# Expert gathers of a two-block transformer kernel: u and v of an index in turn, without pauses, in groups of four

## The chip, the core and the metric

The kernel runs on one core of a Trainium2 chip. The metric is the device time of one execution in microseconds. All arrays are float32.

## What is computed

Two transformer blocks run one after the other over 256 tokens of width 1024. The first ends in a product-key expert layer (PEER), the second in a mixture of 32 experts. The change touches the PEER layer alone:

```python
def one_block(hb):                                   # 128 tokens
    q = (hb @ w_q).reshape(128, 8, 2, 128)
    sc = einsum('thcd,hcnd->thcn', q, sub_keys)      # 8 heads, 2 halves, 128 keys
    s1, i1 = top_k(sc[:, :, 0], 16); s2, i2 = top_k(sc[:, :, 1], 16)
    cand_s = (s1[..., :, None] + s2[..., None, :]).reshape(128, 8, 256)
    top_s, pos = top_k(cand_s, 16)
    idx = i1 * 128 + i2 at pos                       # 16 of 16384 experts
    g = softmax(top_s)
    act = gelu(einsum('thkd,td->thk', u_tab[idx], hb))
    return einsum('thk,thkd->td', g * act, v_tab[idx])
```

For each of 2 tiles of 128 tokens, 8 heads and 16 choices k, every token needs one row of 4 KB of u_tab and one of v_tab: 256 gathers of each table, 128 rows (0.5 MB) each, 268 MB in all.

## The kernel before

**Stages.** One program: block one with its weights streamed by SP (SyncE) through five slots of a ring in SBUF (a slot is 16 KB a partition, a unit 2 MB), the gather stage, block two with more units through the same slots, and last the experts, whose weights are streamed too. The units are numbered in the order of loading; unit n goes to slot n mod 5, and the last five of block one (four of w_peer_q, one of sub_keys) lie in slots 0 to 4 while TensorE computes the scores for the search. A sixth slot is not used by units then.

**Gather stage.** The order is written out by hand on each engine, and engines meet only in semaphores. A head of a tile is g = 8 tile + head; two heads make a pair, `par` is the head in the pair. Everything runs in program order on its engine:

- POOL (lines 681 to 712) waits for the indices of a head (`s_route`), copies them to `idx_now`, tells so (`s_taken`), issues the 16 u gathers and then the 16 v gathers, one indirect DMA each. A u gather waits until the dot on its row buffer is done (`s_dot`; eight buffers), a v gather until TensorE has used its buffer (`s_pv`; sixteen buffers). Ahead of each k with k % 4 == 2 POOL sets a small tile `spacer` to zero and waits for it (lines 695 to 696 and 705 to 706). The v gathers of the first head wait for the last use of ring slots 1 to 4 by block one (line 703), the u gathers from k = 4 on for that of slot 0.
- DVE (lines 1762 to 1800) forms the dot of each gathered u row with the token's row (`dot_rows`, one instruction per k over 1024 elements, line 1766), multiplies gelu by the softmax weight (`weights`), and does the search for the next pair in between: `best_keys` (two rounds of the eight best of 128, line 1558) behind the weights of the first head, `route` (sums, two rounds of the eight best of 256, indices, softmax, line 1576) behind those of the second. The search of the very first head comes before any dot, that of the second between its dots and weights.
- ACT (lines 1293 to 1325) computes gelu over a head's 16 dots, 16 diagonal matrices with the weights on the diagonal (line 1303), and the exponentials for the softmax. Before it come its copies for block one, the last of them the scores of key 7.
- TensorE (lines 908 to 919) waits for the 16 diagonals of a head (`s_diag`), then for each v gather, and adds diagonal times v rows to two PSUM banks: two matmuls of 512 columns for each k.
- SP (lines 616 to 628) loads the first unit of block two into slot 0 when all 256 dots are done (line 619), and the next four when the v rows in their slots have been used.

## Time and profile before

| | us |
|---|---|
| median of 3 runs | 2437.82 |
| lowest and highest run | 2437.38, 2440.33 |
| span of the profiled execution | 2439.8 |
| busy: TensorE, weight loads | 2067.6, 1173.3 |
| busy: DVE, ACT, POOL | 981.6, 552.4, 519.0 |
| 256 gathers of u on POOL, line 698: busy, mean of one | 240.9, 0.941 |
| 256 gathers of v on POOL, line 708: busy, mean of one | 244.2, 0.954 |
| 256 dots on DVE, line 1766: busy, mean of one | 312.5, 1.221 |
| 256 diagonals on ACT, line 1303: busy | 76.5 |
| matmuls on gathered rows, line 905, x1024: busy, mean of one | 480.7, 0.633 |

How to read it: the slices of the page cut the span in 40 parts of 61 us each; a digit is the tenth of the slice in which an engine was busy. PE is TensorE, PEld its weight load, SP is SyncE. The gathers go through the software queue q0, the loads of weights through the hardware queue q1, and both are served by the same 16 DMA engines. The span is 2.0 us above the median of the runs.

### The profile page before, as it was taken

The page shows a single profiled execution, that of the slowest core. Times are in us where ns is not written, and L with a number is a line of the kernel's source. Part 1 is how long each engine was busy: PE and PEld are TensorE (multiplying, and loading weights), DVE is VectorE, ACT ScalarE, POOL GpSimd, SP SyncE. Part 2 cuts the span into 40 slices and gives each one's busy share as a digit, 9 for nine tenths or more (in the row PEclk, how much of TensorE's full clock was granted, in tenths as well). Part 3 has the DMA queues.
Part 4 walks back from the last instruction along what each step waited for, and adds up shares of the span by engine and source line. Part 5 has one row for each costly group of instructions (what it writes and reads, how often), then busy time and mean ns, then how long its engine had stood idle before and what let it go on. Part 6 is the DMA issues. An engine that isn't in the chain of part 4 may idle for free.

```text
span 2439.8 us, 27459 instructions
## 1 busy us (share of the span) xinstructions
PE 2067.6 (85%) x8940; PEld 1173.3 (48%) x8941; DVE 981.6 (40%) x2190; ACT 552.4 (23%) x1000; POOL 519.0 (21%) x688
## 2 busy tenths in 40 slices
PE   8999999757746756755899969999999999999997
PEld 7777888423322322322478854444444444444443
DVE  5955555465665576464065341111111111111113
ACT  4635201221011112011214222222222222222221
POOL 0000002466666666666100000000000000000000
PEclk9999999978878877887999979999999999999999
DMA  7352585699999999999633318699999999999995
GB/s 293 138 207 81 214 359 208 248 362 361 360 352 369 358 364 354 358 349 369 248 138 139 142 74 366 257 430 429 428 428 429 428 428 429 428 429 428 429 429 219
DMA packets 111686, 784.32 MB, mean 321 GB/s; under 512 B 13040, under 2 KB 13296, under 8 KB 80144
## 3 DMA queue, kind: packets, MB, share of 16 engines
q1 hardware_dynamic: 37904, 515.18, 51.0%
q0 software_dynamic: 73728, 268.47, 29.7%
q8 instruction: 28, 0.46, 0.1%
q14 instruction: 26, 0.21, 0.0%
HBM read 782.55 MB, written 1.05 MB: 321 GB/s over the span
## 4 chain that ended last, share of the span: by engine, by line
PE 47%; issue 2%; DVE 1%; DMA 1%; ACT 1%; DVEq 0%; POOL 0%; ACTq 0%; POOLq 0%
PE ps L746 42%; PE ps L905 3%; PE ps L1104 1%; DMA ring<-in_peer_v,arena 1%; PE ps L1135 0%; PE ps L1136 0%; DVE arena L1806 0%; PE ps L1061 0%; DVE ring L2054 0%; ACT arena L1344 0%; DVE arena L2056 0%; DVE ring L2055 0%; ACT arena L1416 0%; ACT arena L1341 0%; DVE arena L1808 0%
## 5 line engine op out<-in xcount | busy, mean ns | idle before, releaser
L746 PE MATMUL ps<-ring,arena 128*64 128x512 f32 (+2 forms) x3336 | 748.4, 588 | 44.4 <-issue 40.5
L905 PE MATMUL ps<-ring,arena 128*128 128x512 f32 x1024 | 480.7, 633 | 266.1 <-issue 187.7
L746 PEld LDWEIGHTS ps<-ring,arena 128*64 128x64 f32 (+1 forms) x3336 | 263.0, 140 | 502.6 <-issue 498.1
L746 PE MATMUL ps<-arena,ring 128*128 128x256 f32 x2208 | 492.5, 382 | 8.6 <-ACT arena L1353 3.7
L905 PEld LDWEIGHTS ps<-ring,arena 128*128 128x128 f32 x1024 | 206.8, 204 | 538.7 <-issue 530.8
L746 PEld LDWEIGHTS ps<-arena,ring 128*128 128x128 f32 x2208 | 419.3, 191 | 75.3 <-issue 13.6
L1766 DVE CUSTOM_DVE_ANT_0 ring<-ring,ps 128x1024 f32<-128x1024 f32 x256 | 312.5, 1221 | 241.1 <-DMA ring<-in_peer_u,arena 226.1
L2027 DVE TENSOR_TENSOR arena<-ps,arena 128x512 f32<-128x512 f32 x66 | 45.7, 692 | 647.6 <-PE ps L1104 647.6
L1456 ACT COPY arena<-ps 128x512 f32<-128x512 f32 (+1 forms) x198 | 108.4, 548 | 728.3 <-PE ps L746 672.2
L708 POOL DMA_INDIRECT ring<-in_peer_v,arena x256 | 244.2, 954 | 135.8 <-issue 105.0
L698 POOL DMA_INDIRECT ring<-in_peer_u,arena x256 | 240.9, 941 | 130.2 <-issue 74.8
L746 PE MATMUL ps<-arena 128*128 128x128 f32 (+6 forms) x1486 | 222.6, 306 | 28.2 <-DVEq L2003 13.6
L746 PEld LDWEIGHTS ps<-arena 128*128 128x128 f32 (+2 forms) x1486 | 197.4, 198 | 45.6 <-issue 21.8
L1295 ACT ACTIVATE arena<-arena 128x16 f32<-128x16 f32 x16 | 4.9, 308 | 569.2 <-issue 318.6
L690 POOL COPY arena<-arena 128x16 uint32<-128x16 uint32 x16 | 3.3, 203 | 390.3 <-POOLq L689 390.2
L1303 ACT ACTIVATE arena<-arena 128x128 f32<-128x128 f32 x256 | 76.5, 388 | 5.6 <-DVE arena L1773 3.4
L905 PE MATMUL ps<-arena 64*128 64x512 f32 (+2 forms) x312 | 75.2, 579 | 2.6 <-ACTq L1430 1.0
L1527 DVE CUSTOM_DVE_ANT_0 ring<-ring,arena 128x1024 f32<-128x1024 f32 x48 | 56.0, 1222 | 3.1 <-DVE arena L1680 0.7
L1832 DVE SCALAR_TENSOR_TENSOR arena<-arena 128x256 f32<-128x256 f32 x120 | 50.2, 481 | 1.6
L1819 DVE TENSOR_SCALAR arena<-arena 128x128 f32 (+1 forms) x68 | 18.5, 288 | 78.4 <-issue 73.4
L727 POOL MEMSET arena<- 128x128 f32 x1 | 0.2, 205 | 216.5 <-DVEq L1941 216.5
L1456 ACT ACT_TABLE_LOAD x33 | 42.3, 1283 | 16.3 <-ACT arena L1456 15.2
(332 smaller groups left out, 1101.3 us busy)
## 6 DMA issues: line engine op xcount, KB each, us to landing
ring<-in_w_exp SPq DMA_DIRECT2D x192, 2048.0 KB, 17.1
ring<-in_w_in SPq DMA_DIRECT2D x24, 2048.0 KB, 8.3
ring<-in_w_ada SPq DMA_DIRECT2D x12, 2048.0 KB, 8.9
ring<-in_w_out SPq DMA_DIRECT2D x4, 2048.0 KB, 7.8
ring<-in_w_peer_q SPq DMA_DIRECT2D x4, 2048.0 KB, 12.4
ring<-in_w_br_rnn SPq DMA_DIRECT2D x4, 1280.0 KB, 9.5
ring<-in_w_br_attn SPq DMA_DIRECT2D x2, 2048.0 KB, 13.8
ring<-in_peer_u,arena POOLq DMA_INDIRECT x256
```

The lines of the kernel that those rows point to most:

```text
L698: pool.indirect_dma_start(out=u_rows[k % 8], out_offset=None, in_=a["peer_u"], in_offset=bass.IndirectOffsetOnAxis(ap=idx_now[:, par, k:k ...
L708: pool.indirect_dma_start(out=v_gath[k], out_offset=None, in_=a["peer_v"], in_offset=bass.IndirectOffsetOnAxis(ap=idx_now[:, par, k:k + 1] ...
L746: return pe.matmul(o, l, r, start=start, stop=stop)
L905: return pe.matmul(o, l, r, start=start, stop=False, skip_group_check=True)
L1104: last = pe.transpose(ps[:, EXPERT_BANK[job], j * P:(j + 1) * P], z_sb[:, n, j * P:(j + 1) * P], ident)
L1303: last = fn(diag[:, par, k, :], ident, ACT.Copy, scale=wts[:, par, k:k + 1])
L1456: own(act.copy(dst, src))
L1527: own.mark(dve.tensor_tensor_reduce(w[:, j, :], w[:, j, :], c_row, 1.0, 0.0, ALU.mult, ALU.add, mod[:, m:m + 1]))
L1766: dve.tensor_tensor_reduce(u_rows[k % 8], u_rows[k % 8], h2_rows[tile], 1.0, 0.0, ALU.mult, ALU.add, dots[:, par, k:k + 1]).then_inc(s_dot, 1)
L1819: own.mark(ts(dst[:, t, :], numbers, slot_of[:, t, at_e], None, ALU.is_equal))
L1832: own.mark(stt(conv[:, c, :], src, w, conv[:, c, :], ALU.mult, ALU.add))
L2027: own(tt(dst.rearrange("p j (h s) -> p j h s", h=2), ps[:, bank, :].rearrange("p (j h s) -> p j h s", j=4, h=2), bias.unsqueeze(3).to_broa ...
```

## The change

A gather buffer is now a pair of 8 KB: u in its first half, v in its second, in sixteen slots instead of eight u buffers and sixteen v buffers. Twelve of the pairs lie in the ring, four in the arena. POOL issues u and v of an index one behind the other, both counting on one semaphore of that slot (`uv_full`), with a single wait (TensorE has used the slot) and no spacer. DVE, ACT and TensorE work in groups of four k: four dots, gelu, weights, four diagonals, eight matmuls. The search is cut into six pieces that stand behind the dots and before the weights of a group. The very first two heads are searched one by one before any dot. SP loads each unit of block two when the two pairs in its ring slot have been used by the last head. Work per gather, dot, diagonal and matmul is the same.

```diff
+GROUP = 4
-        carve("P", CR, T)
+        hole = carve("P", CR * T)
-        spacer = carve("P", 2 * TOPK)
-        u_rows = [ring[:, i * D:(i + 1) * D] for i in (20, 21, 22, 23, 0, 1, 2, 3)]
-        v_gath = [ring[:, (4 + i) * D:(5 + i) * D] for i in range(16)]
+        in_ring = [ring[:, i * 2 * D:(i + 1) * 2 * D] for i in range(12)]
+        in_arena = [hole[:, 0:2 * D]] + [carve("P", 2 * D) for _ in range(3)]
+        uv_rows = in_ring[10:12] + in_ring[0:2] + in_arena + in_ring[2:10]
+        ring_place = {0: 2, 1: 8, 2: 10, 3: 12, 4: 14}
+        n_groups = TOPK // GROUP
# SP
-                if n == n_first:
-                    sp.wait_ge(s_dot, 8 + TT * PH * TOPK)
-                elif n < n_first + RING:
-                    sp.wait_ge(s_pv, 17 + TT * PH * TOPK - 4 * (RING - 1 - n % RING))
+                if n < n_first + RING:
+                    sp.wait_ge(s_pv, 17 + (TT * PH - 1) * TOPK + ring_place[n % RING] + 2)
# POOL
                         for k in range(TOPK):
+                            for s, place in ring_place.items():
+                                if k == place:
+                                    unit_free(pool, last_in_slot(s, n_first))
                             if k == 4:
-                                unit_free(pool, last_in_slot(0, n_first))
-                            if k % 4 == 2:
-                                own(pool.memset(spacer, 0.0))
-                            own.mark(pool.wait_ge(s_dot, i * (2 * TOPK) + TOPK * g + k + 1))
-                            pool.indirect_dma_start(
-                                out=u_rows[k % 8], ..., in_=a["peer_u"], ...).then_inc(u_full[k % 8], 16)
-                        for s in range(1, RING):
-                            unit_free(pool, last_in_slot(s, n_first))
-                        for k in range(TOPK):
-                            if k % 4 == 2:
-                                own(pool.memset(spacer, 0.0))
+                                A.filled(pool, "ss2")
                             own.mark(pool.wait_ge(s_pv, i * (2 * TOPK) + TOPK * g + k + 2))
-                            pool.indirect_dma_start(
-                                out=v_gath[k], ..., in_=a["peer_v"], ...).then_inc(v_full[k], 16)
+                            pool.indirect_dma_start(out=uv_rows[k][:, 0:D], ..., in_=a["peer_u"],
+                                                    in_offset=at_k).then_inc(uv_full[k], 16)
+                            pool.indirect_dma_start(out=uv_rows[k][:, D:2 * D], ..., in_=a["peer_v"],
+                                                    in_offset=at_k).then_inc(uv_full[k], 16)
# TensorE
-                        pe.wait_ge(s_diag, i * 2 + g + 1)
                         for k in range(TOPK):
-                            pe.wait_ge(v_full[k], i * 32 + 16 * (g + 1))
+                            if k % GROUP == 0:
+                                pe.wait_ge(s_diag, i * (2 * n_groups) + g * n_groups + k // GROUP + 1)
# ACT
             for tile in range(TT):
                 if tile == 0:
-                    gelu_dots(0, 0, 0)
                     act.wait_ge(s_soft_in, 2)
                     fn(top_s[:, 1, :], top_s[:, 1, :], ACT.Exp).then_inc(s_soft, 1)
...
                 with act.Fori(1 - tile, PH // 2 - tile) as i:
                     for par in range(2):
-                        gelu_dots(tile, par, i)
-                        diagonals(tile, par, i)
+                        for j in range(n_groups):
+                            gelu_dots(tile, par, j, i)
+                            diagonals(tile, par, j, i)
+                        if par == 0:
+                            next_exponentials(i + tile * (PH // 2) + 1)
# DVE, first two heads
-            best_keys(0, slice(0, 1))
-            route(0, slice(0, 1))
+            for h in range(2):
+                head = slice(h, h + 1)
+                best_keys(0, 0, head); best_keys(0, 1, head); best_pairs(0, head); best_pairs(1, head)
...
+                soften(0, head); part_of_route(0, head); part_of_route(1, head); give_route(head)
+                normalise(1 + h, head)
# DVE, dots of a group
+                for k in range(j * GROUP, (j + 1) * GROUP):
+                    dve.wait_ge(uv_full[k], i * 64 + 32 * (g + 1))
+                    last = dve.tensor_tensor_reduce(uv_rows[k][:, 0:D], uv_rows[k][:, 0:D], h2_rows[tile], ...,
+                                                    dots[:, par, k:k + 1])
+                last.then_inc(s_dots, 1)
# DVE, first pair of tile 0: head 1
+                    dot_rows(0, 1, 0, 0); best_keys(1, 0); best_keys(1, 1); weights(0, 1, 0, 0)
+                    dot_rows(0, 1, 1, 0); best_pairs(0); best_pairs(1); soften(1); weights(0, 1, 1, 0)
+                    dot_rows(0, 1, 2, 0); part_of_route(0); weights(0, 1, 2, 0)
+                    dot_rows(0, 1, 3, 0); part_of_route(1)
                     dve.wait_ge(s_taken, 2)
+                    give_route(); weights(0, 1, 3, 0); normalise(3)
# DVE, loop over the other pairs
+                    dot_rows(tile, 0, 0, i); best_keys(after, 0); weights(tile, 0, 0, i)
+                    dot_rows(tile, 0, 1, i); best_keys(after, 1); weights(tile, 0, 1, i)
+                    dot_rows(tile, 0, 2, i); best_pairs(0); weights(tile, 0, 2, i)
+                    dot_rows(tile, 0, 3, i); best_pairs(1); soften(after); weights(tile, 0, 3, i)
+                    dot_rows(tile, 1, 0, i); part_of_route(0); weights(tile, 1, 0, i)
+                    dot_rows(tile, 1, 1, i); part_of_route(1)
                     dve.wait_ge(s_taken, i * 2 + tile * PH + 2)
+                    give_route(); weights(tile, 1, 1, i)
+                    for j in (2, 3):
+                        dot_rows(tile, 1, j, i); weights(tile, 1, j, i)
+                    normalise(after + 2)
```

(Statements that stand on lines of their own in the kernel are joined by ";" here. `best_keys(p, half)` and `best_pairs(half)` find the first or the second eight of sixteen, `part_of_route(c)` turns a position into the key of half c, `give_route` writes the indices for POOL, `soften` and `normalise` are the two sides of the softmax around ACT's exponential.)

## Rows read from the trace of the kernel before

**Rows 1.** Slices of the page, 40 over the span: two engines, bytes moved.
```profile
PE   8999999757746756755899969999999999999997
POOL 0000002466666666666100000000000000000000
GB/s 293 138 207 81 214 359 208 248 362 361 360 352 369 358 364 354 358 349 369 248 138 139 142 74 366 257 430 429 428 428 429 428 428 429 428 429 428 429 429 219
```
**Rows 2.** Windows: length, busy PE, PEld, DVE, ACT, POOL (count), clock, DMA share, GB/s.
```profile
480.00:1080.00 600.00, 382.20 (x832) 166.02 (x831) 367.23 (x864) 86.80 (x244) 406.12 (x527) 0.82 0.97 359
1160.00:1167.00 7.00, 7.00 (x18) 3.11 (x17) 0.00 (x0) 0.00 (x0) 3.99 (x6) 1.00 1.03 415
1500.00:2400.00 900.00, 859.86 (x4514) 385.73 (x4510) 153.55 (x341) 198.06 (x279) 0.00 (x0) 1.00 0.98 417
```
**Rows 3.** Timeline of POOL, 502 to 517 us: start, duration, instruction, [idle before it].
```profile
502.87 0.14 POOL L706 MEMSET arena<- 128x32 f32 x1
503.81 0.94 POOL L708 DMA_INDIRECT ring<-in_peer_v,arena  x1 [0.80 <-issue]
505.05 0.94 POOL L708 DMA_INDIRECT ring<-in_peer_v,arena  x1 [0.30 <-issue]
...
510.79 0.93 POOL L708 DMA_INDIRECT ring<-in_peer_v,arena  x1 [0.30 <-issue]
511.72 0.21 POOL L690 COPY arena<-arena 128x16 uint32<-128x16 uint32 x1
512.83 0.97 POOL L698 DMA_INDIRECT ring<-in_peer_u,arena  x1 [0.91 <-issue]
...
516.07 0.94 POOL L698 DMA_INDIRECT ring<-in_peer_u,arena  x1 [0.88 <-POOLq L697]
```
**Rows 4.** Waits of POOL, 466 to 1166 us: total, times, longest.
```profile
POOL ring L708 <- PE ps L905: 4.7, 9, 0.8
POOL ring L698 <- DVE arena L1766: 4.2, 8, 0.9
```
**Rows 5.** Timeline: first u gather and first dot of heads 1 and 15.
```profile
466.46 0.97 POOL L698 DMA_INDIRECT ring<-in_peer_u,arena  x1 [0.90 <-issue]
471.73 1.22 DVE L1766 CUSTOM_DVE_ANT_0 ring<-ring,ps 128x1024 f32<-128x1024 f32 x1 [18.30 <-DMA ring<-in_peer_u,arena]
...
1120.78 0.97 POOL L698 DMA_INDIRECT ring<-in_peer_u,arena  x1 [0.90 <-issue]
1126.12 1.22 DVE L1766 CUSTOM_DVE_ANT_0 ring<-ring,ps 128x1024 f32<-128x1024 f32 x1 [22.09 <-DMA ring<-in_peer_u,arena]
```
**Rows 6.** Queues from 1160 to 1167 us, the only one with packets.
```profile
q0 software_dynamic: 794, 2.90, 102.8%
```
**Rows 7.** End of the stage: timeline of ACT, POOL and PE, and one window.
```profile
1150.39 4.78 ACT L1303 ACTIVATE arena<-arena 128x128 f32<-128x128 f32 x16 [0.24 <-issue]
1164.77 0.94 POOL L708 DMA_INDIRECT ring<-in_peer_v,arena  x1 [0.30 <-issue]
1187.25 6.44 PE L905 MATMUL ps<-ring,arena 128*128 128x512 f32 x8 [3.58 <-DMA ring<-in_peer_v,arena]
1188.00:1192.00 4.00, 4.00 (x6) 1.67 (x5) 0.00 (x0) 0.00 (x0) 0.00 (x0) 0.50 0.04 17
1206.37 29.64 PE L746 MATMUL ps<-arena,ring 128*128 128x256 f32 x128 [3.70 <-ACT arena L1353]
```
**Rows 8.** DVE: the dots (min, median, max ns), search of a pair (windows).
```profile
L1766 DVE CUSTOM_DVE_ANT_0 ring<-ring,ps x256: 1220/1221/1223, 399.1 to 1148.5; 128x1024 f32<-128x1024 f32 x128
681.50:694.95 13.45, 11.48 (x35) 0.65 0.96 365
447.10:453.45 6.35, 5.89 (x35) 0.63 0.87 312
```
**Rows 9.** Start of the stage, timeline: first u and v gathers, DVE's wait.
```profile
394.51 1.13 POOL L698 DMA_INDIRECT ring<-in_peer_u,arena  x1 [1.07 <-POOLq L697]
443.24 0.94 POOL L708 DMA_INDIRECT ring<-in_peer_v,arena  x1 [26.05 <-PE ps L746]
446.28 0.17 DVE L1611 TENSOR_REDUCE arena<-arena 128x1 f32<-128x16 f32 x1 [10.15 <-ACT arena L1310]
```

234 lines of the change are left out of this document (140 added, 94 removed).

## Prediction

> **What bounds the kernel now.** I read the slices of the page first. POOL is busy only in slices 7 to 20, and there TensorE drops to 4 to 7 tenths while the GB/s line stands near 360 [rows 1]. This is the gather stage, some 790 us of the span; the stages behind it wait for its result, so what it loses or gains moves the end one for one. By the windows, DVE is busy 61%, PE 64% at a granted clock of 0.82, ACT 14% and POOL 68% between 480 and 1080 us [rows 2]. No compute engine is full. That leaves the transfers, and the question on which everything rests is whether the 16 DMA engines or POOL's issuing sets their pace. The DMA share of 0.97 in the same row suggests the engines.
>
> The timeline of POOL says otherwise. A plain step from one gather to the next is 0.94 for the instruction and 0.30 of idle time, 1.245 by the starts. A spacer makes it 0.94 + 0.14 + 0.80 = 1.88 ahead of a v gather and 1.96 ahead of a u gather (0.88 idle), and the copy of the next head's indices 0.93 + 0.21 + 0.91 = 2.05 [rows 3]. A head's 32 gathers make 23 plain steps, 4 + 4 with a spacer, and 1 copy: 28.6 + 7.8 + 7.5 + 2.0 = 46.0 us; the first gathers of two heads start at 466.46 and 512.83, 46.4 apart [rows 3, 5]. POOL hardly waits for slots: 4.7 us for PE and 4.2 for DVE in 700 us [rows 4]. And the gathers land soon: the first u gather of a head is issued at 466.46 and, 14 heads later, at 1120.78, its dot starts at 471.73 and 1126.12: 5.3 us later both times [rows 5]. A queue that were too slow for its issuer would fall behind over 650 us; this one does not. So POOL, with its pauses, sets the pace and the DMA engines follow.
>
> How fast they could go is seen once. From 1160 to 1167 the gathers queue up behind a weight load, the hardware queue is silent, and the software queue alone moves 2.90 MB at 415 GB/s, while POOL still issues [rows 2, 6]. A gather is 128 rows of 4 KB, 0.524 MB: 1.26 us at 415 GB/s, against 1.46 at the stage's 359. The high DMA share at 359 GB/s is then packets that wait for work with their clock running; that is my inference.
>
> Here a rule of the Trainium skill speaks against the change. The page "HBM Reference" (its table of bandwidths) gives an effective 358 GB/s per core, half of a stack's 716, and the stage sits on that figure; it adds that a core that streams alone measures about 425. By the first figure nothing is to be had from faster issuing. By that rule the trace disagrees: 415 GB/s for gathers, 417 for the expert weights [rows 2]. The rule is one of the rivals below, with its time from rows.
>
> **The change part by part.** The sum runs from the first gather of the second head to the end of the stage; before, that gather is issued at 466.46 and the last one, 479 steps later, at 1164.77 [rows 5, 7]: 698.3 us, 1.458 each.
>
> *Pauses gone, u and v in turn.* A head has 31 plain steps and one copy: 31 x 1.245 + 2.05 = 40.6 us, 1.27 a gather. The steps of before add up to 46.0 a head, yet 698.3 x 32 / 479 is 46.65, so 0.6 a head (0.02 a gather) is irregular; I keep it: 1.29. One wait for two gathers instead of one each may shorten the 0.30 or not; the bounds are 0.94 (no gap) and 1.245, and I take 1.245, since that is what all plain steps show. The DMA floor is 1.26, so a faster POOL would gain only down to that. 479 x 1.29 = 617.9 us: 80.4 less. In all 16 slots a gather now finds one free: a pair is held from issue to landing (5.3), until its group of four has landed (up to three pairs, 7.7), for a dot (1.22 [rows 8]), a piece of search (up to 4), gelu and weights (0.7, between the last dot and the first diagonal), four diagonals (4.78 / 4 = 1.2 [rows 7]) and at most 8 matmuls (6.4 at 1.2 GHz [rows 7]): 27 us, against 41 until the slot's turn comes again.
>
> *Start.* Today u gathers of head 0 go out from 394.51, and the v gathers stand still until 443.24 for the last ring slot [rows 9]. The new order fills four arena slots and slot 5 and 0 at once and takes the others as TensorE leaves them (400 to 443): head 0 is fully issued by about 447, 17 us sooner than 465.36. But DVE now searches both heads before its first dot, and the second normalise waits for an exponential that ACT issues only behind its last key copy: today DVE stands there until 446.28 [rows 9]. ACT has the first gelu less ahead of it, so the dots start at about 446. Four dots (5.0), gelu and weights (0.7), diagonals (1.3) and the first pair of matmuls (1.6 at 1.2 GHz) free the first slot: head 1's first gather at 455, **11.5 us earlier** than 466.46. POOL is idle for some 8 us before it. DVE then needs 5.7 us per uncovered group, which is under the 10.3 that POOL needs to issue one.
>
> *The first routes.* In the first pair of heads the next route is given only behind the last dots of head 1. Head 1 is issued from 455 to 495.5; its last pair lands near 500, a dot and the second half of the routing (3 + 0.6 us by the sum of its rows, [rows 8]) put the route at 504, and POOL needs it at 496: **+8 us**, once. In the loops the route comes two groups earlier, ahead of POOL's need.
>
> *Search in pieces.* The same instructions as before: 6.3 us of keys and 13.3 of pairs and routing for two heads [rows 8]. With 32 dots of 1.25 that is 60 us of DVE per 81 us of gathers. Each piece is 2.9 to 4 us and stands behind four dots, 9 us of a group's 10.3. Covered at no cost; if the gathers came at 1.15 us each, the cover would be gone.
>
> *End.* Today SP has asked for four weight units by the time the last gather is issued, and they share the queue with it: issue at 1164.77, matmul at 1187.25, 22.4 us where the steady lag is 5.3 [rows 5, 7]. Now slot 0's load starts behind the first group of the last head and the others behind the third and fourth, so one unit of 2 MB (5.1 us at 415 GB/s) lies beside the last gathers: 10.4 us, **12 us less**. The next stage reads the units from 12.7 us after the last matmul (1206.37 - 1193.69), one per 7.4 (29.64 / 4) [rows 7], and four units take about 20 us at 417 GB/s, the first of them under way by then; it should not wait. Behind the last landing come now a dot, gelu, weights, four diagonals and 8 matmuls: 1.25 + 0.7 + 1.3 + 6.4 = 9.7, against 6.5 today [rows 7]: **+3**.
>
> Sum: -80.4 - 11.5 + 8 - 12 + 3 = **-93 us**. The profiled execution's span is 2439.8; the median of the runs is 2437.8, 2 us under it. I carry the difference over: 2437.8 - 93 = **2345 us**. Its own range goes by the pace: 1.266 (the DMA floor) and no wait for routes give -20, so 2325; 1.34 gives +24, so 2369.
>
> **The rivals.**
>
> *A. The ceiling of the stage is HBM's.* Then gathers stay at the 359 GB/s of the stage, 1.46 each, and only start and end gain: 479 x 1.46 = 699, so +1 - 11.5 + 4 (half of the route's wait is covered by a backlog) - 12 + 3 = -15.5: **2422 us**. For it: a steady 360 GB/s in all slices. Against it: the 415 GB/s and the constant lag. The page named above says this for a core whose neighbour is busy.
>
> *B. POOL or the loop is slower than the bare steps.* DVE's search and POOL's descriptor writing meet more often, or the hand-offs DVE, ACT, DVE, ACT, PE of each group hold slots longer than 27 us. A pace of 1.38 gives 479 x 0.09 = 43 more: **2388 us**. For it: 0.6 us a head are irregular already. Against it: POOL's waits for PE and DVE add up to 9 us.
>
> *C. Slower: two tables in turn.* Today 16 gathers in a row read one table, now each reads the other one at the same indices; no stretch of the trace does that, and none shows a queue kept full for longer than some 10 us. If a full, alternating queue moves less, all 479 steps pay. It decides from 1.29 + 93 / 479 = 1.484 us, 353 GB/s, on; at 330 GB/s (1.59) it is 479 x 0.30 - 93 = +51: **2489 us**. Against it I have only that DMA served 415 GB/s behind a backlog, of one table.
>
> *D. The pauses go and nothing moves,* since POOL is held by slots at just the old pace: needs a hold of 46 us, 19 more than my sum. 2437 us.
>
> **How the numbers follow.** My forecast 0.70, B 0.12, A 0.09, C 0.06, D 0.03. Forecast and B reach from 2325 to about 2400 and hold 0.82; I give 2323 to 2402. The kernel can be told from no change from about 0.2%, 5 us. Faster: forecast, B, A, 0.90 after rounding for what I have not thought of; same 0.03; slower 0.07.
>
> **What the profile would show.** The first test is the step of POOL's timeline: 1.245 throughout with 2.04 at each head, and 40.6 to 41.3 us from one copy of indices to the next. GB/s in the stage: 405 or more in my case, 375 to 395 in B, near 360 in A with gathers much longer than 0.94 us or POOL waiting for PE, under 353 in C. DMA idle for some 5 to 8 us before 460 and again near 500. The last matmul near 1100 instead of 1193.7. TensorE in the stage: bursts of 8 matmuls with pauses, the granted clock at or under 0.82, much of it at 1.2 GHz; harmless as long as 8 matmuls (6.4 us) fit in a group's 10.3. The prediction fails if the lag from issue to landing grows while POOL waits for slots: then the engines, not POOL, set the pace.

## The result, and the profile after

The kernel after takes **2347.2 us** (median of 4 runs, 2346.5 to 2348.0), the kernel before 2437.7: a ratio of 0.9631, with an interval of 0.9618 to 0.9644. That is 90.5 us less. The profiled execution's span is 2345.1, 94.7 under that of before.

The page of after: its head, three lines of the slices, the groups of gathers and dots, and the median time from issue to landing of the u gathers (last line; its last number).

```profile
span 2345.1 us, 27078 instructions
PE 2090.4 (89%) x8940; PEld 1175.9 (50%) x8941; DVE 977.5 (42%) x2238; ACT 569.1 (24%) x1046; POOL 499.9 (21%) x560
PE   8999999868877777876999889999999999999996
POOL 0000002557777777773000000000000000000000
GB/s 305 140 213 64 179 358 254 288 330 410 410 410 409 409 409 410 410 407 379 108 144 108 144 217 257 420 429 429 428 428 428 429 429 429 428 428 428 429 429 215
L1790 DVE CUSTOM_DVE_ANT_0 ring<-ring,ps 128x1024 f32<-128x1024 f32 x192 | 231.9, 1220 | 153.5 <-DMA ring<-in_peer_v,arena 153.0
L699 POOL DMA_INDIRECT ring<-in_peer_u,arena x192 | 182.7, 951 | 87.4 <-issue 47.3
L701 POOL DMA_INDIRECT ring<-in_peer_v,arena x192 | 179.9, 937 | 59.8 <-issue 55.8
ring<-in_peer_u,arena POOLq DMA_INDIRECT x192, 6.8
```

Against [rows 1] the GB/s line of the gather stage stands at 409 to 410 where it wandered between 349 and 369, the stage is a slice and a half shorter, and PE works at 7 to 8 tenths in it. Gathers and dots cost what they cost before: 0.94 to 0.95 and 1.22 us each. Only the idle time between them went.

Windows of after (length, busy PE, PEld, DVE, ACT, POOL, granted clock, DMA share, GB/s), the stage without its ends; it answers to the first line of [rows 2].

```profile
500.00:1060.00 560.00, 430.57 (x875) 179.13 (x874) 369.73 (x898) 102.58 (x289) 413.90 (x449) 0.89 1.01 404
```

Timeline of POOL in after, at the change from one head to the next; it answers to [rows 3].

```profile
829.30 0.94 POOL L701 DMA_INDIRECT ring<-in_peer_v,arena  x1 [0.30 <-issue]
830.24 0.21 POOL L689 COPY arena<-arena 128x16 uint32<-128x16 uint32 x1
831.43 0.97 POOL L699 DMA_INDIRECT ring<-in_peer_u,arena  x1 [0.99 <-POOLq L697]
832.71 0.94 POOL L701 DMA_INDIRECT ring<-in_peer_v,arena  x1 [0.31 <-issue]
833.95 0.93 POOL L699 DMA_INDIRECT ring<-in_peer_u,arena  x1 [0.30 <-PE ps L895]
```

The plain step is 833.95 - 832.71 = 1.24, as before, and the one with the copy 831.43 - 829.30 = 2.13 (2.05 before). From 451.31, the first gather of head 1, to 1075.66, the last of all, the 479 steps take 624.35 us. One stop of 11.9 us is in it, so the pace is 612.5 / 479 = 1.279 us.

Start of the stage in after: DVE's wait for the last exponential, the first dot, TensorE's first group and head 1's first gather. It answers to [rows 9] and the first lines of [rows 5]. The last line is the first route that POOL has to wait for: its idle time of 11.87 us is the stop.

```profile
439.51 0.17 DVE L1625 TENSOR_REDUCE arena<-arena 128x1 f32<-128x16 f32 x1 [34.66 <-ACT arena L1306]
440.38 1.22 DVE L1790 CUSTOM_DVE_ANT_0 ring<-ring,ps 128x1024 f32<-128x1024 f32 x1 [0.22 <-issue]
446.93 8.71 PE L895 MATMUL ps<-ring,arena 128*128 128x512 f32 x16 [5.69 <-ACT arena L1296]
451.31 0.97 POOL L699 DMA_INDIRECT ring<-in_peer_u,arena  x1 [5.68 <-POOLq L697]
...
502.67 0.20 POOL L689 COPY arena<-arena 128x16 uint32<-128x16 uint32 x1 [11.87 <-DVEq L1540]
```

End of the stage in after, timeline; it answers to [rows 7].

```profile
1075.66 0.94 POOL L701 DMA_INDIRECT ring<-in_peer_v,arena  x1 [0.31 <-issue]
1089.14 1.22 DVE L1790 CUSTOM_DVE_ANT_0 ring<-ring,ps 128x1024 f32<-128x1024 f32 x1 [1.25 <-DMA ring<-in_peer_v,arena]
1092.27 7.13 PE L895 MATMUL ps<-ring,arena 128*128 128x512 f32 x16 [1.59 <-ACT arena L1296]
```

The last matmul of the stage ends at 1092.27 + 7.13 = 1099.4, where it was 1193.7: all of the gain lies ahead of this point. What comes behind it takes 1245.7 us of the span, and took 1246.1.

One thing to know before comparing start times between executions: the first gather of all, which comes right behind block one and the first head's search, starts at 394.51 in before and at 392.54 in after. From that gather to the end of the span it is 2045.3 us in before and 1952.6 in after, 92.7 less.

### The profile page after: what moved, and what is told of

Same layout as the page of the kernel before. It is cut to its first block, busy times and chain, and to the rows that moved or that the text cites. A ratio compares the mean times of both kernels' runs of the same rounds, so it can differ in the third digit from the quotient of the medians.

```text
span 2345.1 us, 27078 instructions
## 1 busy us (share of the span) xinstructions
PE 2090.4 (89%) x8940; PEld 1175.9 (50%) x8941; DVE 977.5 (42%) x2238; ACT 569.1 (24%) x1046; POOL 499.9 (21%) x560
## 4 chain that ended last, share of the span: by engine, by line
PE 71%; POOL 7%; DMA 7%; issue 6%; DVE 6%; ACT 3%; DVEq 0%; POOLq 0%; ACTq 0%; SPq 0%
PE ps L736 58%; PE ps L895 10%; DMA ring<-in_peer_v,arena 4%; POOL ring L699 2%; POOL ring L701 2%; DMA arena<-in_peer_v,arena 2%; PE ps L1095 1%; POOL arena L699 1%; POOL arena L701 1%; ACT arena L1296 1%; DVE ring L1790 1%; DMA ring<-in_sub_keys 0%; DVE arena L1740 0%; ACT arena L1241 0%; PE ps L1126 0%
## 5 line engine op out<-in xcount | busy, mean ns | idle before, releaser
L895 PE MATMUL ps<-ring,arena 128*128 128x512 f32 x768 | 389.9, 667 | 125.8 <-ACT arena L1296 125.8
L895 PEld LDWEIGHTS ps<-ring,arena 128*128 128x128 f32 x768 | 160.9, 215 | 352.4 <-issue 194.2
L1790 DVE CUSTOM_DVE_ANT_0 ring<-ring,ps 128x1024 f32<-128x1024 f32 x192 | 231.9, 1220 | 153.5 <-DMA ring<-in_peer_v,arena 153.0
L736 PE MATMUL ps<-arena 128*128 128x128 f32 (+6 forms) x1486 | 220.9, 304 | 28.1 <-DVEq L2059 13.6
L895 PE MATMUL ps<-arena 64*128 64x512 f32 (+2 forms) x568 | 194.1, 597 | 26.3 <-ACT arena L1296 23.7
L699 POOL DMA_INDIRECT ring<-in_peer_u,arena x192 | 182.7, 951 | 87.4 <-issue 47.3
L701 POOL DMA_INDIRECT ring<-in_peer_v,arena x192 | 179.9, 937 | 59.8 <-issue 55.8
L895 PEld LDWEIGHTS ps<-arena 128*128 128x128 f32 (+1 forms) x568 | 78.0, 191 | 118.1 <-issue 77.8
L1790 DVE CUSTOM_DVE_ANT_0 arena<-arena,ps 128x1024 f32<-128x1024 f32 x64 | 76.7, 1220 | 34.0 <-DMA arena<-in_peer_v,arena 33.4
L699 POOL DMA_INDIRECT arena<-in_peer_u,arena x64 | 60.7, 948 | 19.5 <-issue 15.6
L701 POOL DMA_INDIRECT arena<-in_peer_v,arena x64 | 60.2, 940 | 19.5 <-issue 19.2
## 6 DMA issues: line engine op xcount, KB each, us to landing
ring<-in_w_peer_q SPq DMA_DIRECT2D x4, 2048.0 KB, 10.4
```

What stands on the lines that cost most here:

```text
L699: pool.indirect_dma_start(out=uv_rows[k][:, 0:D], out_offset=None, in_=a["peer_u"], in_offset=at_k).then_inc(uv_full[k], 16)
L701: pool.indirect_dma_start(out=uv_rows[k][:, D:2 * D], out_offset=None, in_=a["peer_v"], in_offset=at_k).then_inc(uv_full[k], 16)
L736: return pe.matmul(o, l, r, start=start, stop=stop)
L895: return pe.matmul(o, l, r, start=start, stop=False, skip_group_check=True)
L1790: last = dve.tensor_tensor_reduce(uv_rows[k][:, 0:D], uv_rows[k][:, 0:D], h2_rows[tile], 1.0, 0.0, ALU.mult, ALU.add, dots[:, par, k:k + 1])
```

## The experiments

**1. The pauses alone.** The kernel before, with its layout, its two tables one behind the other and its groups of sixteen, without the spacer.

> The kernel before with nothing changed but the eight spacers per head taken out of POOL's stream: u buffers, v buffers, the run of 16 u gathers and then 16 v gathers, whole heads and the unbroken search stay. Theory P (the pauses alone set the pace): a head takes 31 x 1.245 + 2.05 = 40.6 to 41.3 us instead of 46.4, so 479 steps x (1.458 - 1.28) = 85 us less: 2353 us, between 2347 and 2362. Rival L (pairs in slots, turns and groups are needed to keep DVE, ACT and PE up with faster gathers): POOL waits for its eight u buffers or its v buffers, a head takes 44 us or more, 2400 us or more.

```diff
-                per = 2 * (2 + 2 * TOPK + 2 * TOPK // 4)
+                per = 2 * (2 + 2 * TOPK)
...
-                            if k % 4 == 2:
-                                own(pool.memset(spacer, 0.0))
...
-                            if k % 4 == 2:
-                                own(pool.memset(spacer, 0.0))
```

Measured: **2356.5 us** (2351.8 to 2358.1, 4 runs), ratio 0.9657 (0.9636 to 0.9678). Slices of this kernel (bytes moved) and the largest of its waits of POOL in the stage (total, times, longest):

```profile
GB/s 304 115 215 86 164 367 254 233 409 408 402 410 410 409 408 400 410 400 355 112 140 108 146 188 261 420 429 428 428 429 428 428 429 429 428 428 429 429 428 210
...
POOL ring L696 <- DVE arena L1762: 14.5, 42, 2.0
```

Eight small instructions a head, taken out of POOL's stream, give 81 of the 90.5 us, and up to 410 GB/s with them. Pairs, turns, groups and the search in pieces are worth some 9 us together.

Where the 9 us lie can be read from the two traces. The old layout costs little in the steady state: the 479 steps from head 1's first gather on take 616.2 us here and 612.5 in after without its stop, 4 us more. (The 14.5 us that POOL waits for one of the eight u buffers, where it waited 4.2 [rows 4], say less than they seem to: each of these waits holds the 0.30 us of idle time that every plain step has, 42 times here and 8 times there.) Head 1 starts 66.9 us after the first gather of all, where it is 58.8 in after, and after loses these 8 us again, and more, in its stop before head 2, which this kernel doesn't have. What is left is the end: from the last issue to the end of the span it is 1278.3 us here and 1269.5 in after, 9 less.

**2. The pauses put back.** The kernel after, with a spacer ahead of every fourth gather.

> The changed kernel with eight spacers per head put back (one behind every four gathers); all else as changed. Theory P: a head takes 40.65 + 8 x 0.70 = 46.2 us, 479 steps grow by 0.17 each, +80 us: 2427 us, between 2415 and 2436. Rival L (the layout and groups carry the gain): within 20 us of the changed kernel, 2347 to 2367.

```diff
+        spacer = carve("P", 2 * TOPK)
...
-                per = 2 * (2 + TOPK)
+                per = 2 * (2 + TOPK + TOPK // 2)
...
+                            if k % 2 == 1:
+                                own(pool.memset(spacer, 0.0))
```

Measured: **2428.8 us** (2424.6 to 2433.8, 10 runs), ratio 0.9965 (0.9954 to 0.9976). A window of the stage, the spacer with the gather behind it, and the page's median from issue to landing:

```profile
500.00:1040.00 540.00, 382.05 (x743) 157.75 (x741) 324.75 (x815) 89.10 (x246) 361.08 (x470) 0.85 0.96 353
...
700.93 0.15 POOL L699 MEMSET arena<- 128x32 f32 x1
701.98 0.94 POOL L702 DMA_INDIRECT ring<-in_peer_u,arena  x1 [0.90 <-POOLq L700]
...
ring<-in_peer_u,arena POOLq DMA_INDIRECT x192, 5.6
```

Seen from this side the pauses are 81.6 us, and everything else 8.9. The two experiments agree within the scatter of the runs, so the parts add up: no sign that they help or hinder one another.

**3. The turns undone.** The layout and the groups of after, with sixteen u gathers and then sixteen v gathers into the same slots; DVE waits for u alone, TensorE for v, once a group.

> The changed kernel, but POOL issues the 16 u gathers of a head and then its 16 v gathers, into the same slots; DVE waits for u alone, TensorE for the v rows of a group of four. Theory P: the order of the two tables costs and gives nothing; POOL still steps by 1.245, a slot is held for about 20 + 5.3 + 3.7 + 6.4 = 35 us of the 41 until its turn, so 2347 within 6 us. Rival T (rival C of the prediction in either direction: turns between the two tables at one index change what the DMA engines move): a difference of more than 10 us at a GB/s in the stage other than 404, with the lag from issue to landing changed by over 1 us.

```diff
-        uv_full = [sem(f"uv_rows_loaded_{k}") for k in range(TOPK)]
+        u_full = [sem(f"u_rows_loaded_{k}") for k in range(TOPK)]
+        v_full = [sem(f"v_rows_loaded_{j}") for j in range(TOPK // GROUP)]
...
                             pool.indirect_dma_start(out=uv_rows[k][:, 0:D], out_offset=None, in_=a["peer_u"],
-                                                    in_offset=at_k).then_inc(uv_full[k], 16)
+                                                    in_offset=at_k).then_inc(u_full[k], 16)
+                        for k in range(TOPK):
+                            at_k = bass.IndirectOffsetOnAxis(ap=idx_now[:, par, k:k + 1].bitcast(U32), axis=0)
                             pool.indirect_dma_start(out=uv_rows[k][:, D:2 * D], out_offset=None, in_=a["peer_v"],
-                                                    in_offset=at_k).then_inc(uv_full[k], 16)
+                                                    in_offset=at_k).then_inc(v_full[k // GROUP], 16)
...
+                            if k % GROUP == 0:
+                                pe.wait_ge(v_full[k // GROUP], i * (2 * 16 * GROUP) + 16 * GROUP * (g + 1))
...
-                    dve.wait_ge(uv_full[k], i * 64 + 32 * (g + 1))
+                    dve.wait_ge(u_full[k], i * 32 + 16 * (g + 1))
```

Measured: **2364.5 us** (2363.5 to 2366.4, 4 runs), ratio 0.9699 (0.968 to 0.9718): 17 more than after, where I had expected no difference. A window, head 1's first gather, POOL's waits from there on, and the page's median from issue to landing:

```profile
500.00:1040.00 540.00, 386.82 (x844) 167.86 (x842) 357.94 (x895) 101.00 (x284) 389.36 (x422) 0.86 1.01 397
...
464.07 0.97 POOL L700 DMA_INDIRECT ring<-in_peer_u,arena  x1 [0.97 <-POOLq L698]
...
POOL ring L700 <- PE ps L898: 25.4, 49, 0.8
...
ring<-in_peer_u,arena POOLq DMA_INDIRECT x192, 6.0
```

Head 1's first gather starts 12.8 us later than in after (10.7 counted from the first gather of all), since no v gather of head 0 can go out before all its u gathers, and those need the last ring slot. The stop before head 2 is 8.6 us shorter in return. The rest are waits of POOL for slots: a slot now waits from its u gather until its v gather, sixteen steps later, has landed and been used. In heads 1 to 15 some 38 gathers have more idle time before them than the plain 0.30, mostly 0.78 and 17 us too much together; in after it is one gather, 1.3 us. So the turns are worth something by how long a slot is held and by an earlier start. That the DMA engines should care which table comes next, rival C, has nothing for it: the 397 GB/s are fewer than the 403 of after over the same window, but gathers land sooner (6.0 against 6.8 us), so it is POOL that issues less and not the queue that is slower.

**4. Fewer bytes.** The kernel after, with v gathers of 512 columns (half rows of a view of the table with 2 KB rows); both halves of the result are formed from them. Part of the computation is thus changed, and a quarter of the bytes of the stage is gone. The number of gathers, dots and matmuls is the same.

> The changed kernel with v gathers of 512 columns (rows of 2 KB out of the table seen as twice as many rows) in place of 1024; TensorE multiplies the same 512 columns for both halves of the output, so the output is another one. Bytes of the stage fall by a quarter. Theory P: POOL's steps are the bound, every head takes 40.65 instead of 40.65 to 41.9 us (mean 41.0), the stage is some 5 us shorter and the end 3 us: 2339 us, between 2333 and 2344. Rival D (the DMA engines at some 410 GB/s hold the stage and POOL is kept back by them): with 0.39 MB per gather on average the pace could fall towards 1.0 us and the time by 20 us or more, 2325 or less.

```diff
-                            pool.indirect_dma_start(out=uv_rows[k][:, D:2 * D], out_offset=None, in_=a["peer_v"],
+                            pool.indirect_dma_start(out=uv_rows[k][:, D:D + 512], out_offset=None, in_=a["peer_v"].rearrange("n (h c) -> (n h) c", h=2),
...
-                            add(ps[:, 2 * tile + 1, :], diag[:, par, k, :], uv_rows[k][:, D + 512:2 * D])\
+                            add(ps[:, 2 * tile + 1, :], diag[:, par, k, :], uv_rows[k][:, D:D + 512])\
```

Measured: **2345.9 us** (2342.9 to 2348.2, 4 runs), ratio 0.9616 (0.9596 to 0.9637), 1.3 under after and not to be told from it. The window of the stage, its slices, and the median from issue to landing:

```profile
500.00:1040.00 540.00, 411.02 (x847) 171.62 (x847) 359.31 (x883) 99.83 (x280) 399.55 (x430) 0.90 0.89 301
...
GB/s 305 113 215 90 155 378 230 209 263 307 304 311 298 309 307 306 305 300 340 108 144 108 144 217 259 420 428 429 428 428 428 429 428 429 429 428 429 428 428 211
...
ring<-in_peer_u,arena POOLq DMA_INDIRECT x192, 4.8
```

With the load of the engines down from 404 to 301 GB/s the stage is as long as before. So POOL's own issuing is a bound too. The few us that I had expected to come back did not: I had put the irregular 0.6 us of a head down to the engines, and they are not theirs. The GB/s line says it as well: it wanders from 298 to 311, as it wandered in [rows 1], where POOL set the pace, while after's stands still at 409 to 410.

The traces also show where much of the irregular part is. A few gather instructions last 1.0 to 1.4 us on POOL instead of 0.94: 9 of them in heads 1 to 15 of after, 14 in this experiment. Every one of the 9 stands beside instructions of DVE's search, 7 of them beside its operations on 128x512 elements; none of the 358 gathers that a dot overlaps in after is one of them. Timeline of after:

```profile
572.36 0.69 DVE L1609 TENSOR_TENSOR arena<-arena 128x512 f32<-128x512 f32 x1
572.59 1.28 POOL L699 DMA_INDIRECT ring<-in_peer_u,arena  x1 [0.31 <-issue]
573.13 0.69 DVE L1611 TENSOR_TENSOR arena<-arena 128x512 f32<-128x512 f32 x1
```

That the search causes them is not shown by an experiment; they fit the first half of rival B, at a small price (3 us in all in after).

**5. Groups undone on DVE.** In the loops (12 of the heads) the weights of a head are formed only behind its sixteen dots, in the layout of after.

> The changed kernel, but in the loops (6 of 8 pairs of heads) DVE forms the weights of all four groups only behind the last dots of the head and the search pieces; pairs in slots, turns, no pauses stay. Theory H (a slot holding u and v is given back late unless diagonals follow each group): the first slot is held from issue for 38 (15 pairs issued) + 5.3 (landing) + 1.25 (dot) + up to 4 (piece) + 0.7 + 1.3 + 1.6 = 48 to 52 us against the 41 of its turn, POOL waits for PE, some 50 us a head in 12 heads: 2347 + 12 x 9 = 2455 us, between 2425 and 2485, slower than the kernel before. Rival N (groups bring nothing, POOL's steps decide): 2347 within 5 us.

```diff
                     best_keys(after, 0)
-                    weights(tile, 0, 0, i)
                     dot_rows(tile, 0, 1, i)
...
-                    weights(tile, 0, 3, i)
+                    for j in range(n_groups):
+                        weights(tile, 0, j, i)
...
-                    weights(tile, 1, 1, i)
-                    for j in (2, 3):
-                        dot_rows(tile, 1, j, i)
+                    dot_rows(tile, 1, 2, i)
+                    dot_rows(tile, 1, 3, i)
+                    for j in range(n_groups):
                         weights(tile, 1, j, i)
```

Measured: **2512.7 us** (2509.4 to 2514.4, 4 runs), ratio 1.0309 (1.0292 to 1.0325): slower than the kernel before by 75 us, 58 more than I had put on it. Timeline of a head's end: the last dot, the first weights, the first diagonals and POOL's next gather.

```profile
549.80 1.22 DVE L1790 CUSTOM_DVE_ANT_0 ring<-ring,ps 128x1024 f32<-128x1024 f32 x1 [1.26 <-DMA ring<-in_peer_v,arena]
553.63 0.16 DVE L1797 TENSOR_TENSOR arena<-arena 128x4 f32<-128x4 f32 x1 [0.21 <-issue]
553.91 1.28 ACT L1296 ACTIVATE arena<-arena 128x128 f32<-128x128 f32 x4 [33.87 <-DVE arena L1797]
...
559.83 0.97 POOL L699 DMA_INDIRECT ring<-in_peer_u,arena  x1 [16.81 <-POOLq L697]
```

POOL has issued the whole head and stands for 12 to 17 us in each; the heads take 53 to 57 us by their first gathers. The price is larger than expected for two reasons. The last pair of this head is on its dot 7.9 us after its issue where I took 5.3 for the landing. And the way from the first matmul to POOL's next gather is long: TensorE starts at 555.24 and POOL at 559.83, 4.6 us later, where I took 1.6. This is the other side of experiment 1. The pair layout with sixteen slots is harmless only because slots come free in fours; with slots freed by whole heads it turned the change into a loss.

**6. A shorter start.** The kernel after, with ACT's second exponential behind its copy of q 3 rather than behind its last key copy, the search of the second pair between the dots of head 0, and its route given behind head 0.

> The changed kernel with its first pair of heads reordered: ACT computes the second exponential behind its copy of queries 3 instead of behind the last key copy, DVE then does the dots of two groups and the whole search of pair 1 while TensorE still computes keys, and the route of pair 1 is given behind head 0. Theory S (the two waits at the start are real and nothing else takes their place): head 1's first gather at 448 instead of 451.3 and no 11.9 us stop before head 2, 15 us less than the changed kernel: 2332, between 2328 and 2338. Rival: DVE's or ACT's queue is late elsewhere (gelu of head 0 waits for ACT's last key copy, so DVE stands before its weights) and POOL stops at head 1 instead: 2342 or more.

```diff
                     act.sem_inc(s_pq, 1)
+                    if i == 3:
+                        act.wait_ge(s_soft_in, 2)
+                        fn(top_s[:, 1, :], top_s[:, 1, :], ACT.Exp).then_inc(s_soft, 1)
...
-                    for j in range(n_groups):
-                        dot_rows(0, 0, j, 0)
-                        weights(0, 0, j, 0)
-                    dve.wait_ge(s_ps, n_pairs)
-                    dot_rows(0, 1, 0, 0)
+                    dot_rows(0, 0, 0, 0)
+                    dot_rows(0, 0, 1, 0)
+                    dve.wait_ge(s_ps, 3)
                     best_keys(1, 0)
                     best_keys(1, 1)
...
                     give_route()
-                    weights(0, 1, 3, 0)
+                    for j in range(n_groups):
+                        dot_rows(0, 1, j, 0)
+                        weights(0, 1, j, 0)
```

Measured: **2330.6 us** (2327.8 to 2334.3, 5 runs), ratio 0.9566 (0.9553 to 0.9579), 16.6 under after, as expected. Head 1's first gather starts at 445.04 and there is no stop before head 2. Of the 6.3 us by which it starts sooner, 2.9 are block one's (the first gather of all is at 389.60, not 392.54) and 3.3 the edit's; with the 11.9 of the stop that makes 15.2. Both waits that I had found at the start were on the path, at full price.

**7. One weight unit less beside the last gathers.** Experiment 6, and SP asks for the unit of slot 0 only when the last pair has landed.

> As e6_start, and SP loads the first unit of block two only when the last pair of gathers has landed. Theory: the last gathers land 5 us earlier, since no 2 MB unit shares the queue with them, and block two still finds its units in time: 5 us less than e6_start, 2327, between 2323 and 2333. Rival: the five units now come 5 us later and block two waits for them, which takes the gain back: the same as e6_start within 1.5 us.

```diff
                 name, i, words = units[n]
+                if n == n_first:
+                    sp.wait_ge(uv_full[TOPK - 1], 32 * TT * PH)
                 if n < n_first + RING:
```

Measured: **2329.3 us** (2326.8 to 2330.9, 5 runs), ratio 0.9554 (0.9541 to 0.9567). Timelines: experiment 6's last gather and last dot, then the same of experiment 7.

```profile
1057.58 0.93 POOL L701 DMA_INDIRECT ring<-in_peer_v,arena  x1 [0.30 <-issue]
1071.21 1.22 DVE L1791 CUSTOM_DVE_ANT_0 ring<-ring,ps 128x1024 f32<-128x1024 f32 x1 [1.25 <-DMA ring<-in_peer_v,arena]
```

```profile
1063.35 0.94 POOL L703 DMA_INDIRECT ring<-in_peer_v,arena  x1 [0.30 <-issue]
1072.09 1.22 DVE L1793 CUSTOM_DVE_ANT_0 ring<-ring,ps 128x1024 f32<-128x1024 f32 x1 [1.26 <-DMA ring<-in_peer_v,arena]
```

From the last gather to the last dot it is 8.7 us instead of 13.6: the unit of 2 MB did cost its 5 us. In the medians only 1.3 us of it can be seen. The first gather of a kernel, which none of these edits touches, starts anywhere between 389.6 and 395.6 in these executions, by how block one went. That scatter hides it. Counted from the first gather of all, the two profiled executions differ by more: 681.6 and 677.3 us to the last dot, 1936.4 and 1933.4 to the end of the span. With one trace of each and medians 1.3 apart, how much of the 5 us is a gain of the kernel is not settled; the rival, that block two waits for its units, is neither needed nor excluded.

**8. The copy of indices off POOL's path.** Experiment 7, with the second head's indices copied ahead of the last pair of the first head.

> As e7_start_tail, and POOL copies the indices of the second head of each pair ahead of the last pair of gathers of the first head, so that no gather waits for that copy: one step of 2.05 becomes 1.245 in 8 of 16 heads. Theory P (POOL's steps are the only bound): 8 x 0.8 = 6.5 us less than e7_start_tail, 2321. Rival F (the DMA engines have a floor of their own of about 1.275 us per gather, just above POOL's 1.245, since the lag from issue to landing grows by 0.03 us a step within each head and the 0.8 us pauses at the heads let it recover): 0 to 2 us less, 2325 to 2327, and the lag grows on over two heads to above 7 us.

```diff
-                        pool.wait_ge(s_pv, i * (2 * TOPK) + TOPK * g + 1)
-                        own.mark(pool.wait_ge(s_route, i * 2 + g + 1))
-                        own(pool.tensor_copy(idx_now[:, par, :].bitcast(U32), route_idx[:, par, :].bitcast(U32)))
+                        if par == 0:
...
+                        else:
+                            own.settle()
...
+                            if par == 0 and k == TOPK - 1:
+                                pool.wait_ge(s_pv, i * (2 * TOPK) + TOPK * g + k + 2)
+                                own.mark(pool.wait_ge(s_route, i * 2 + g + 2))
+                                own.mark(pool.tensor_copy(idx_now[:, 1, :].bitcast(U32), route_idx[:, 1, :].bitcast(U32)))
```

Measured: **2329.9 us** (2326.6 to 2331.5, 5 runs), ratio 0.9556 (0.9543 to 0.9569): nothing, as rival F said, though POOL needs less for its steps, 1.265 us each from head 1 on against 1.279 in experiment 7. Timeline: a head's last v gather early and late in the stage, and the dot on its pair; then the median from issue to landing.

```profile
489.44 0.93 POOL L710 DMA_INDIRECT ring<-in_peer_v,arena  x1 [0.30 <-issue]
496.57 1.22 DVE L1800 CUSTOM_DVE_ANT_0 ring<-ring,ps 128x1024 f32<-128x1024 f32 x1 [1.33 <-DMA ring<-in_peer_v,arena]
...
975.29 0.94 POOL L710 DMA_INDIRECT ring<-in_peer_v,arena  x1 [0.30 <-DVEq L1550]
990.91 1.22 DVE L1800 CUSTOM_DVE_ANT_0 ring<-ring,ps 128x1024 f32<-128x1024 f32 x1 [1.34 <-DMA ring<-in_peer_v,arena]
...
ring<-in_peer_u,arena POOLq DMA_INDIRECT x192, 9.3
```

The way from issue to dot grows from 7.1 to 15.6 us, and the stage's slices show 409 to 410 GB/s as in after: what POOL issues sooner lies in the queue. This is the sign of a queue slower than its issuer, which [rows 5] did not show. The floor is 0.524 MB / 410 GB/s = 1.28 us a gather.

## Why the prediction was right, and where it was not

The cause was the one foretold: POOL's pauses set the pace of the stage, the transfers had room, and the gain lies in the pace. By its terms, as the predicted and the measured change of the span:

| term | predicted | measured | from |
|---|---|---|---|
| pace, 479 steps | -80.4 | -85.8 | 1.279 each for 1.458 |
| start of head 1 | -11.5 | -15.2 | 451.31 for 466.46; 2.0 of it is block one's |
| first route | +8 | +11.9 | the stop before 502.67 |
| end, last issue to last dot or matmul | -12 | -9.0 | 13.5 for 22.5 |
| behind the last landing | +3 | +3.8 | 1099.40 - 1089.14 = 10.3 for 6.4 |
| sum | -93 | -94.3 | last matmul: 1099.4 for 1193.7 |

**Pace.** I took 1.29, the bare steps plus the irregular 0.02. What stands there is 1.279, so half of the irregular part went with the pauses. But the step on which I had the engines in reserve ("the DMA floor is 1.26, so a faster POOL would gain only down to that") was nearer than I thought. The floor was read from seven microseconds with 415 GB/s [rows 6]; held over the stage it is 410, or 1.28, and POOL's own steps make 31 x 1.24 + 2.13 = 40.6 a head, or 1.27, and 1.28 with its few long instructions. The two bounds lie within one per cent of each other. Experiments 4 and 8 each move one of them away and gain nothing. Which of them holds after back can't be told from its trace. Timeline of after, a head's last v gather and the dot on its pair, at head 4 and at head 13:

```profile
624.78 0.94 POOL L701 DMA_INDIRECT ring<-in_peer_v,arena  x1 [0.31 <-issue]
631.98 1.22 DVE L1790 CUSTOM_DVE_ANT_0 ring<-ring,ps 128x1024 f32<-128x1024 f32 x1 [1.32 <-DMA ring<-in_peer_v,arena]
...
993.07 0.94 POOL L701 DMA_INDIRECT ring<-in_peer_v,arena  x1 [0.30 <-issue]
999.97 1.22 DVE L1790 CUSTOM_DVE_ANT_0 ring<-ring,ps 128x1024 f32<-128x1024 f32 x1 [1.32 <-DMA ring<-in_peer_v,arena]
1002.51 1.22 DVE L1790 CUSTOM_DVE_ANT_0 ring<-ring,ps 128x1024 f32<-128x1024 f32 x1 [1.31 <-DMA ring<-in_peer_v,arena]
```

7.2 us at first, 9.4 later, and the dots at the end of a head follow each other every 2.54 to 2.55 us, each released by a DMA. The lag doesn't grow evenly: measured like this it is 6.8 to 7.3 us in heads 2 to 7, 8.2 in head 8, 9.4 to 9.8 in heads 9 to 13 and 8.4 in head 14, while the last u gather of these heads lands in 6.8 to 8.0 us. Why the v gathers take longer in heads 9 to 13 no run shows. I had named as what would make the prediction fail a lag that grows while POOL waits for slots. A part of the first came, small; the second did not.

**Start and first route.** Both were right in kind and mis-sized, against each other. Timelines of ACT, before and then after: what stood ahead of the exponential for which DVE waits, and that exponential.

```profile
443.12 1.28 ACT L1295 ACT_TABLE_LOAD   x1 [0.17 <-ACT arena L1285]
444.74 1.28 ACT L1310 ACT_TABLE_LOAD   x1
...
439.26 0.22 ACT L1306 ACTIVATE arena<-arena 128x16 f32<-128x16 f32 x1 [0.19 <-ACT arena L1276]
```

DVE had its exponential at 439.5 instead of 446.3. The last key copies did stand in the way, as I had read, but they were done 3.9 us earlier in this execution: luck, as far as the sum goes. The other 2.9 us are the change's: before, ACT's first gelu stood between these copies and the exponential, and with it two table loads of 1.28 us each. I had noted that the gelu goes and put no number on it. Together that made the first dot some 6 us earlier than the 446 that I took. It lost 3 again where I had priced the first pair of matmuls at 1.6 us: from TensorE's start at 446.93 to POOL's gather at 451.31 it is 4.4. I had misread a row there. In the timeline a gather's two matmuls are four records (256 gathers, 1024 records in the table of before; 16 records for a group of four in after), so the 8 records of 6.44 us in [rows 7] are two gathers' matmuls and not a group's, and the first pair costs twice what I took. (A small slip beside it: head 0 fully issued at 447 is 18 us sooner than 465.36 and not 17. Nothing rests on it.)

The stop before head 2 is 11.9 us and not 8, and not because head 1 starts sooner: its dots start sooner too. Head 1's last gather is issued at 489.86 and the dot on it starts at 498.07, 8.2 us later, where I had worked with a landing some 5 us after the issue. Experiment 4 shows the same from the other side: there that gather's dot comes 4.8 us after it and the stop is 8.4. Experiment 6 shows what an earlier head 1 and the missing stop are worth together, 16.6 us in the medians.

**End.** I gave the last gather 10.4 us to land beside one weight unit and it took 13.5. By then the way from the last issue of a head to its dot was 8.4 us (head 14), and no longer the 5.3 of [rows 5]. Experiment 7 takes the unit away and gets 8.7, so the unit's own price, 5 us, was right, and the lag under it was the wrong term. Experiment 2, where the pauses keep the queue short, has 10.3 with the unit. So one figure was mis-sized in the route, in the end and in experiment 5: the 5.3 us is the lag of a head's first gather at the old pace, and the last one of a head waits longer, behind the gathers ahead of it.

**Behind the last landing.** +3 was forecast and +3.8 came, and that is luck. I took 6.4 us for a group's matmuls, from the row misread above. A group is 16 records: they took 7.13 us here, at a granted clock of 1.00, and would take twice the 6.44 us of [rows 7], 12.9, where the clock is 0.50 (an estimate).

**Search in pieces, slots.** No cost, as said: from head 1 on, one gather of after has more idle time before it than a plain step or a copy explains (1.57 us, at head 14; no run shows why). That a slot must come free in fours was in my sum of 27 us of 41. With the matmuls at 12.9 in place of 6.4 that sum is 33, still under 41 (an estimate). Experiment 5 shows that this margin was what the change rested on: it lengthens the hold by the dots of a head and costs 165 us against after.

**Clock.** I forecast "at or under 0.82" in the stage and it is 0.89. I took shorter bursts of matmuls to mean more time at 1.2 GHz. What the rows show: between 500 and 1040 us TensorE stands 12 times before gathered rows in before, 16.8 us each on average, and 41 times in after, 3.0 us each; the granted clock is 0.86 in experiment 1 and 0.85 in experiment 2, so the missing pauses and the groups each go with a higher one. I had called a low clock harmless as long as 8 matmuls fit in a group's 10.3 us. With the 16 records of a group that doesn't hold: at the lower level throughout, a group's 12.9 us (the estimate above) would be more than 10.3, and TensorE would set the pace. The prediction needed a clock well above its own forecast's low end and got it, a rival that neither I nor any experiment priced.

**The rivals.** A, the ceiling: refuted by the 409 to 410 GB/s. The rule of the Trainium skill that stood behind it ("HBM Reference", its table of bandwidths) puts an effective 358 GB/s on each core, which it gives as the share with both cores of a pair streaming; taken as a ceiling for this kernel the trace disagrees, 410 for gathers and 428 to 429 for the expert weights. With its addition for a core that streams alone, some 425, the trace agrees to within a few per cent. B: refuted as a bound, 1.279 for 1.38, though its meeting of DVE's search and POOL is there in small (experiment 4). C: refuted by after itself, which moves 410 GB/s with the tables in turn, as experiment 1 does without; experiment 3 shows that the turns are rather a small gain. D: refuted by 90.5 us.

## What to carry to other kernels

When an issuing engine and the transfers behind it look equally busy, look at the lag from issue to landing over a long stretch: constant and short, the issuer sets the pace and every instruction between its issues is on the path; growing, the queue does. In these traces a GB/s line that wandered belonged to the issuer (before, experiments 1 and 4), and with the queue full (experiment 8) it stood still; but it stands still in after too, where the two bounds meet, so the line alone doesn't tell. A lag is best read at the same place of every round, since the first gather behind a pause waits least. And price a layout together with the order of work that frees its buffers: the same sixteen pairs were worth a few us with groups of four and a loss of 75 us without them. Last, count the records of a timeline row before pricing an instruction by it.

## What the runs showed of the hardware that I had not expected

- **The share of busy DMA engines does not tell how full they are.** It was 0.97 at 359 GB/s [rows 2], 0.96 at 353 in experiment 2, 1.01 at 404 in after, 0.89 at 301 in experiment 4. An eighth more data changed it by 0.04. The Trainium skill says as much ("Perfetto Trace Analysis", in its section on identifying the most-contended engine: with 16 engines occupancy misleads, go by the bandwidth), and the trace agrees.
- **410 GB/s is the most that gathers of 4 KB rows held for long,** flat over eight slices (415 stands over seven microseconds [rows 2]), while the weights of the same kernel load at 428 to 429.
- **From the first matmul of a group to the gather that it releases** it is 4.4 to 4.6 us (446.93 to 451.31, 555.24 to 559.83). In both cases the granted clock is 0.50, TensorE's lower level of 1.2 GHz. A pair's four records end 3.6 and 3.8 us after the start of the first, POOL's wait ends 0.03 later, and its gather starts another 0.78 behind that.
- **Before the exponential ACT loaded a table twice,** 1.28 us each, because a gelu stood between: the order of two short functions cost 2.9 us on the path.
- **An index list copied early** hardly costs POOL anything: in experiment 8 the gathers at 1014.74 and 1016.04 have the copy between them and are 1.30 apart, where a copy that the next gather depends on makes a step of 2.13 out of 1.24.
